# Two projections beside attention computed as seven products of sums instead of eight tiles, in a two-network kernel on one Trainium2 core

## The reference, cut to what matters

```python
# first block, second layer (_odd_mixer), last layer: latents only
def branch(p, attn):
    return (attn * jax.nn.silu(p[..., o_v:])) @ w_out          # p = h @ w_in; o_v: is 2048 columns wide
y = branch(p, _attend(q_of(p[..., :o_q], pos), k, v))

# second block: three merge gates of 2048 columns each, from the same h @ w_in
g_na, g_pool, g_rw = jnp.split(jax.nn.sigmoid(keep(merge_logits)), N_BRANCH, axis=-1)
merged = g_na * (b_na @ w_branch[0]) + g_pool * (b_pool @ w_branch[1]) + g_rw * (b_rw @ w_branch[2])
```

## Time and profile before

| | |
|---|---|
| median of 3 runs | 3873.2 us (3864.82, 3873.74, 3873.2) |
| the profiled execution | 3861.0 us, its span 3859.2 us |
| PE busy | 3607.4 us of the span, 93% |
| DVE busy | 1925.7 us, 50% |
| ACT busy | 680.3 us, 18% |
| granted TensorE clock, mean | 0.983 |
| DMA | 799.05 MB, mean 207 GB/s |
| stage att_c | PE from 1545.0 us to about 1743 us |
| stage att_h | PE from 2418.1 us to about 2570 us |

### The profile page before, as it was taken

One profiled execution on the slowest core, in us unless ns is written; L12 is line 12 of the kernel. 1 busy time (PEld: TensorE's weight loads), 2 busy tenths in 40 slices (PEclk: granted clock), 3 DMA queues, 4 the chain that ended last, 5 costly groups with the idle time before them and its releaser, 6 DMA issues. The chain is left out here.

```text
span 3859.2 us, 60011 instructions
## 1 busy us (share of the span) xinstructions
PE 3607.4 (93%) x24893; PEld 1842.4 (48%) x24893; DVE 1925.7 (50%) x3143; ACT 680.3 (18%) x1365; POOL 560.3 (15%) x801
## 2 busy tenths in 40 slices
PE   8799998899989998999999999898998888989998
PEld 1354443334544446554444444443346666764443
DVE  0399993433346767236646567436533334431411
ACT  0100000121320112331100000335622222221000
POOL 0011111121000001000000011631113223331100
PEclk9999999999999999999999999999999999999999
DMA  8778996784235566325566586657854333335752
GB/s 294 287 279 300 360 370 239 277 324 144 79 141 196 196 228 228 115 89 217 207 238 251 193 324 233 195 178 260 269 164 144 110 101 107 110 109 186 248 193 98
DMA packets 362558, 799.05 MB, mean 207 GB/s; under 512 B 26574, under 2 KB 73702, under 8 KB 357674
## 3 DMA queue, kind: packets, MB, share of 16 engines
q1 hardware_dynamic: 259920, 459.69, 34.9%
q0 software_dynamic: 72736, 274.10, 19.7%
q10 hardware_dynamic: 29634, 61.45, 4.2%
HBM read 686.94 MB, written 108.22 MB: 206 GB/s over the span
## 5 line engine op out<-in xcount | busy, mean ns | idle before, releaser
L1442 PE MATMUL gemm_a_g_ps<-store_w,turned 128*128 128x512 f32 (+1 forms) x1152 | 456.8, 559 | 2.4 <-PEq L205 2.4
L975 DVE SCALAR_TENSOR_TENSOR pmods_acc<-pmods_w,cond,pmods_acc 128x512 f32<-128x512 f32 x540 | 384.5, 749 | 24.2 <-issue 1.3
L1442 PEld LDWEIGHTS gemm_a_g_ps<-store_w,turned 128*128 128x128 f32 x1152 | 209.0, 191 | 249.7 <-issue 249.7
L3171 PE MATMUL scan_g_ps<-store_w,turned 64*64 64x512 f32 x2048 | 290.5, 606 | 14.7 <-DVE outlet_stage L3185 6.9
L1442 PE MATMUL att_a_g_ps<-store_w,turned 128*128 128x512 f32 x512 | 240.2, 599 | 7.0 <-ACT outlet_stage L2919 4.2
L1442 PE MATMUL feat_g_ps<-store_w,turned 128*128 128x512 f32 x384 | 180.3, 618 | 15.9 <-ACT outlet_stage L2454 13.7
L1442 PE MATMUL tail_g_ps<-store_w,turned 128*128 128x512 f32 x384 | 167.0, 597 | 4.7 <-PEq L4002 3.8
L1489 PE MATMUL out_c_g_ps<-store_w,turned 128*128 128x512 f32 x384 | 167.6, 592 | 0.0
L1442 PE MATMUL tail_g_ps<-store_w,tail_branch_t 128*128 128x512 f32 x384 | 165.7, 592 | 0.9 <-ACT tail_branch_t L3927 0.9
L1442 PE MATMUL att_c_g_ps<-store_w,turned_c 128*128 128x512 f32 x256 | 128.7, 604 | 13.5 <-PEq L4002 13.5
L1442 PEld LDWEIGHTS att_a_g_ps<-store_w,turned 128*128 128x128 f32 x512 | 91.5, 191 | 100.1 <-issue 93.4
(11 more groups left out here) (523 smaller groups left out, 5824.8 us busy)
## 6 DMA issues: line engine op xcount, KB each, us to landing
store_w<-in_w_in SPq DMA_DIRECT2D x160, 1024.0 KB, 7.8
pmods_w<-in_w_mod POOLq DMA_DIRECT2D x40, 2048.0 KB, 12.1
store_w<-in_a_w_in SPq DMA_DIRECT2D x48, 1024.0 KB, 11.2
store_w<-in_c_w_in SPq DMA_DIRECT2D x40, 1024.0 KB, 7.4
mods_w<-in_w_mod SPq DMA_DIRECT2D x32, 1024.0 KB, 9.3
store_w<-in_a_w_out SPq DMA_DIRECT2D x32, 1024.0 KB, 6.1
scan_raw<-s_feat SPq DMA_DIRECT2D x112, 256.0 KB, 4.7
s_feat<-feat_o POOLq DMA_DIRECT2D x16, 1536.0 KB, 7.4
```

Source lines behind the costliest of these rows:

```text
L975: v.scalar_tensor_tensor(a, src, x, a, ALU.mult, ALU.add)
L1442: mm = pe.matmul(to, lhs, self.store.slot[i % self.store.NS][:, k, :width], start=first, stop=last)
L3171: mm = pe.matmul(self.ps[r][halves[o], :], self.act_tile(k, tb)[halves[r], halves[o]], self.store.slot[i % self.store.NS][halves[r], k % 4 ...
```

## The change: what it does, and the diff

The four gate chunks become two pairs, the two merge chunks one pair. In both stages PE's product units come from `pair_units` (7 x 8 = 56 for a pair), DVE's list gets the forms and the sums, ACT's list the snaps; silu and sigmoid are applied to the summed results in SBUF. The new items are put into the lists by the count of product units done (`dve_at`, `act_at`): with U = 8 and B the first unit of the pair, form 1 at B, form 2 piece by piece during the second product, form 3 at B + 2U, the sums u2 and u4 and form 4 at B + 3U, the other sums at B + 4U, 5U, 6U and 7U. In att_c the forms are kept in an unused part of `rows_t` and one new tile, and the second pair's results in another part of `rows_t`.

```diff
 def attend_and_project(nc, name, store, outlet, ident, plan, scale, dv, act_tile, projections, lead, last_source, first=None,
-                       mod_jobs=None, rows_t=None, conv_src=None):
+                       mod_jobs=None, rows_t=None, conv_src=None, inputs=None):
...
+        upper_form = sb("upper_form", [P, KD // 4, NCH]) if inputs and plan.gated else None
+        def form_places(n):
+            return [rows_t[:, 3, :].rearrange("p (k c) -> p k c", c=NCH), upper_form]
...
-        order, left = [], sum(len(tbs) for w, tbs, func, dst in projections) * KD
+        job_units = [7 * g.product_units(n) if inputs else len(job[1]) * KD for n, job in enumerate(g.jobs)]
+        order, left = [], sum(job_units)
...
+        result_of = {"y00": (0, 0, 0), "y11": (1, 1, 1), "y01": (2, 0, 1), "y10": (3, 1, 0)}
+        dve_at, act_at = {}, {}
+        for n in range(len(g.jobs) if inputs else 0):
+            U, B, pieces = g.product_units(n), sum(job_units[:n]), store.pieces(g.base + n)
+            for at, item in ([(B, ("T", n, 1))] + [(B + U + U * (x + 1) // pieces, ("T", n, 2, x)) for x in range(pieces)]
+                             + [(B + 2 * U, ("T", n, 3)), (B + 3 * U, ("u", n)), (B + 3 * U, ("T", n, 4)), (B + 4 * U, ("sum", "y01", n)),
+                                (B + 5 * U, ("sum", "y11", n)), (B + 6 * U, ("sum", "y00", n))]):
+                dve_at.setdefault(at, []).append(item)
+            for at, item in ((B + U, ("snap", n, 1)), (B + 2 * U, ("snap", n, 5)), (B + 4 * U + 3, ("result", "y01", n)),
+                             (B + 5 * U + 3, ("result", "y11", n)), (B + 6 * U + 3, ("result", "y00", n))):
+                act_at.setdefault(at, []).append(item)
...
+                dve_order += dve_at.get(done, [])
...
+            def gate_result(key):
+                what, n = key
+                chunk, tb = place_of(key)
+                v.wait_ge(copied, made.index(key) + 1)
+                v.drain()
+                a = rows_t[:, tb, chunk * NCH:(chunk + 1) * NCH]
+                v.tensor_tensor(a, a, slots(n)[result_of[what][0]], ALU.mult).then_inc(gated, 1)
...
             for item in dve_order:
-                if item[0] == "turn":
+                if item[0] == "T":
+                    n, form = item[1:3]
+                    if len(item) == 4:
+                        if item[3] == 0:
+                            forms[n] = g.make_form(v, n, form)
+                        next(forms[n])
+                    else:
+                        for _piece in g.make_form(v, n, form):
+                            pass
+                elif item[0] == "u":
+                    upper(item[1])
+                elif item[0] == "sum":
+                    sum_(*item[1:])
...
-        merge_early, merge_late, merge_last = merge_chunks(0, 2), merge_chunks(2, 8) + merge_chunks(10, 12), merge_chunks(8, 10)
+        merge_early, merge_late, merge_last = in_pairs(merge_chunks(0, 2)), merge_chunks(2, 8) + merge_chunks(10, 12), merge_chunks(8, 10)
...
-        c_gate = c_chunks(LAT, C_GATE, C_END, ACT.Silu)
+        c_gate = in_pairs(c_chunks(LAT, C_GATE, C_END, ACT.Silu))
```

More of the change, by code:

```diff
@@ L1385, in __init__ @@
         if any(self.pair):
-            self.form = [st.enter_context(nc.sbuf_tensor(f"{name}_form{h}", [P, KD // 4, NCH], F32)) for h in range(2)]
+            if not forms:
+                tiles = [st.enter_context(nc.sbuf_tensor(f"{name}_form{h}", [P, KD // 4, NCH], F32)) for h in range(2)]
+                self.forms = lambda n: tiles
             self.snapped, self.added = nc.alloc_semaphore(f"{name}_snapped"), nc.alloc_semaphore(f"{name}_added")
@@ L1505, in make_form @@
             w00, w01, w11, w10 = [store.quarter(load + 2 * x + half)[:, ks, :width] for x in range(4)]
[L1506 removed]
+            made = self.forms(n)[half][:, ks, :width]
             if form == 1:
@@ L2666, in attend_and_project @@
         stat = sb("stat", [P, 4, 4])
+        results = [x[:, :] for x in outlet.stage] + [rows_t[:, 2, n * NCH:(n + 1) * NCH] for n in range(4 if inputs and plan.gated else 0)]
         plan.allocate(sb)
@@ L2743, in attend_and_project @@
                 done += 1
-                ripe += [t for t in range(len(g.tiles)) if plan.gated and g.finished_by(t) == done]
+                dve_order += dve_at.get(done, [])
+                if plan.gated:
+                    ripe += [t for t in range(len(g.tiles)) if g.finished_by(t) == done]
+                    ripe += [item[1:] for item in dve_at.get(done, []) if item[0] == "sum"]
             elif item[0] in ("turn", "score", "value", "rowturn"):
```

99 lines of the change are left out of this document (85 added, 14 removed).

## The result

The changed kernel takes **3882.5 us** (median of 7 runs, 3879.4 to 3885.6), the kernel before 3870.1 us beside it (7 runs, 3864.7 to 3876.6): ratio 1.0033, 95% interval 1.0022 to 1.0044. It is slower, as forecast, but by 12 us and not by 29. The profiled execution took 3879.4 us, its span 3877.6, 18.4 longer than the one of before.

A forecast was written before the change was run, and what follows sets the result against it. It took PE to bound att_c and nearly att_h, with DVE a link in the attention chain. Removed -15.7, waits +31.8, end sums +1.4 and clock +12 made +29.5 us on 3873.2: 3902 us, 8-in-10 range 3879 to 3914.

The forecast's parts named there:

- The room in a step: DVE's idle time between `max_` and `scale_`: 2.2 us in att_c, 0.8 in att_h; anything longer put there delays PE.
- the seven foretold places: Long PE waits behind DVE blocks: att_c start, units 24, 56, 72, 80; att_h units 16, 24; 3 to 5 us each.
- The clock: After six of the seven long waits PE runs at half clock, losing 2.0 us each: +12 us, ends 0 and 16.
- What is removed: Product units taken from PE: 16 in att_c for -14.0 us, 8 in att_h for -1.7; together -15.7 us.
- end: At each stage's end a sum stands between last product and silu or sigmoid: 0.7 us twice, +1.4 us.
- The sum as the whole program's: The two attention stages' terms, +29.5 us in all, were taken as the change of the whole kernel's time.
- A longer time in other stages, for which I have no term: Listed sign that the forecast is wrong: stages other than att_c and att_h take longer; no size given.
- rival 3: About half is absorbed: some blocks run earlier, waits are 16 us, two clock falls; +6 us, 3879 us; chance 0.10.
- The base: The sum was added to the runs' median, 3873.2 us, rather than the profiled execution's 3861.0, which would give 3890.5.
- Rival 1: The waits come in both attention stages but the clock stays up: +17.5 us, 3891 (3882 from the lowest run); chance 0.15.
- None of the four: Rivals 1 and 3, plus DVE hiding the blocks (3859 us, chance 0.08) and late weights (up to 3917, chance 0.07).

The follow-up runs named there:

- narrow_forms: The changed kernel with forms 2, 3 and 4 summed over 8 of 512 columns, so not computing the product: 3841.9 us, ratio to before 0.9944.
- spread: The changed kernel with DVE's form pieces issued one or up to two after each scaling instead of in blocks: 3851.3 us, ratio to before 0.9949.
- only_h: The kernel before with the pair for the merge chunks alone, gate chunks left plain: ratio to before 0.9996.

## Why the prediction was right and wrong

- **The room in a step** (2.2 us between `max_` and `scale_` in att_c, 0.8 in att_h) was read rightly. The blocks turned into waits at the seven foretold places: 5.64, 2.77, 3.31, 4.66, 4.87, 5.00 and 5.80 us against 5.2, 2.8, 3.0, 4.7, 5.0, 4.9 and 5.2. narrow_forms shows that it is the blocks' length, and spread that the same work, taken apart, fits into att_c with 195.5 us against 199.9.
- **The clock.** It fell after six waits, and not after the one of 2.77 us, as forecast. PE was busy at half clock for 27.5 us in those stretches: 13.7 us lost, where 12 was taken. The stretches were longer than the 3.4 and 5.2 us of the earlier trace rows, up to 6.8 us, but PE waited in a part of each. Both stages also began with less time at half clock than before, which gave 1.8 us back; that was in no term and is luck. The rule of the Trainium skill weighed there ("TensorE: Matmul & The Clock Gate", "Loop structure matters more than you think") gave the right side: the trace agrees in six of seven waits.
- **What is removed.** PE's idle time grew by 21.0 us in att_c (4.2 to 25.2), where 20.7 of waits and 0.7 of end were foretold; with 8.8 of clock that is 29.8. The stage grew by 16.5, so 13.3 were removed, for 14.0 taken. In att_h idle time grew by 18.0 and the clock took 3.1; less 15.8, 5.3 were removed, where eight units are 7.0. Of the 18.0, 11.8 are blocks and end, and the rest, 6.2, the units that turned into waits; so the removal brought nothing in att_h, where 1.7 was taken. Mechanism and terms stand, the terms within 2 us each, and the two stages are +32.3 against +29.
- **The sum as the whole program's.** This is the step that failed: the other stages stood in the sum at nothing, without a reason. "A longer time in other stages, for which I have no term" stood in the list of what would prove it wrong, and only as a longer time. The scan came out 13.8 us shorter, and +32.3 - 13.8 with the remaining -0.1 is the measured +18.4 of the two spans. By the executions side by side the total moved by 12 to 13 us, so about 20 us were given back outside of the two stages; 13.8 of them are located, the other 6 are within the scatter of a single execution. The measured 3882.5 lies outside of the forecast's own range, 3888 to 3913, and inside 3879 to 3914 only because that one reached down for rivals 1 and 3, neither of which happened. I had taken it that a stage whose instructions are the same keeps its length. The runs show that it doesn't: the same 8162 matmuls took from 646.5 to 671.3 us, with the stops for PE's instructions and the clock's falls. Why a kernel with pairs has fewer of them is shown for the place of PE's list and open for the rest.
- **The base.** I added the sum to the median of the three runs. Against the profiled execution it made 3890.5, 11 over the measured 3879.4. The median of seven is 3870.1, so 3 us of the miss are the base.
- **The rivals.** Rival 1's 3882 from the lowest run is near the result, and rival 3's 3879 too, for wrong reasons: the clock did not stay up, and the waits were 32 us and not 16. None of the four happened: no block was absorbed, and PE and DVE never waited for `store_w`.

## What to carry to other kernels

An engine that is idle half of the time is no cover for a block of work if it is a link in another engine's chain: measure the room between two links, cut the work into pieces that fit it, and where the room is smaller than a piece, leave the work out of that stage. When long straight-line lists of small instructions are in the program, price a change by stage and not by total: here a stage nobody touched moved by almost as much as each of the stages that were changed, and only_h would have been called free. Before believing half a per cent, put idle instructions ahead of the unchanged kernel, at several counts, and see how far it moves by itself. One profile for each count is not enough where the executions of one kernel differ by as much.

## What the runs showed of the hardware that was not expected

- PE stops for 1 to 3 us with nothing to wait for, at seams 64 matmuls apart in its list (16 KB of instructions). 318 of 332 such stops over 0.9 us end 1.1 to 1.75 us after a packet of instructions has landed; the packet starts late, and does so behind 4 us in which the DMA engines were full (0.97 against 0.21 in the kernel before).
- Idle transpositions 2.7 ms earlier moved the scan by -6.7 to +9.4 us (before) and by -0.8 to +9.0 (changed), in single profiles. The one repeat of a program differed by 0.3 us, and one whole packet more changed the length by 0.7 to 3.1. Over several executions, 56 and 92 of them made the program 10 and 14 us faster.
- After a wait for DVE of 3.3 to 5.8 us the granted clock was 0.54 over 7.5 us in five cases of six and 0.57 over 4.0 us in the sixth; after the 4.0 us wait of the earlier trace rows it had been 0.52 over 3.4.
